# Modulation sums of two streams: one on VectorE, one on GpSimd, with GpSimd's transfers dealt out behind them

## The chip, the core and the metric

The program runs on one core of a Trainium2 chip. The core has a matmul engine (TensorE, PE in the profile), VectorE (DVE), ScalarE (ACT), GpSimd (POOL) and SyncE (SP), which here only issues transfers. The metric is device time of the program in microseconds (us). TensorE's clock is granted in two levels, 1.2 and 2.4 GHz; a stretch's granted clock of 1.00 means 2.4 GHz throughout.

## The reference, cut to what matters

Two layers of a block with three kinds of attention on a latent stream `x` and a context stream `ctx` (256 rows each, 2048 wide, float32), followed by a second block that the change doesn't touch. Each layer begins with a modulation: two vectors, one for each stream, are multiplied with the same matrix `w_ada[l]` of 2048 x 6144.

```python
sc = jax.nn.silu(c)
scc = jax.nn.silu(c_ctx)
shift, scale, gate = jnp.split(sc @ w_ada[l] + b_ada[l], 3, axis=-1)
shift_c, scale_c, gate_c = jnp.split(scc @ w_ada[l] + b_ada[l], 3, axis=-1)
h = rms(x, norm_w[l]) * (1.0 + scale[:, None]) + shift[:, None]
hc = rms(xc, norm_w[l]) * (1.0 + scale_c) + shift_c
u = h @ w_in          # for both streams, the same weights
x = x + gate[:, None] * merge_out(o_a, o_b, o_c, z, w_out[l])
```

The attention of kind A adds a bias table `rpb_a` of relative positions.

## The kernel before

**Weights.** All weight matrices stream through a ring of five slots in SBUF (`raw_ring`), 512 KB a chunk: 128 partitions x 1024 float32. SyncE issues the loads in one fixed order and waits before each for the slot's last user. A chunk of kind S (w_in, w_out) is split in two float32r parts: ScalarE casts it to `w_hi` (L666), VectorE subtracts to `w_lo` in place (L672), and TensorE multiplies three times (L703), 24 matmuls of 512 columns for four tiles of rows. VectorE prepares a chunk two ahead of the one that TensorE multiplies.

**Modulation blocks.** The matrices w_ada are cut in blocks of 512 columns, each of eight chunks. The first eight blocks run on TensorE at the start. The other 16 (numbers 8 to 23) are hosted: one chunk of w_ada (kind M) stands behind one chunk of kind S in the ring, as the list `PLACES` says. Twelve of these blocks serve both streams (`streams(n) == 2`): they lie behind win0 b 0 to 5, z0 b 1 to 3 and wout0 b 0 to 3, all in layer 0. The last four serve one stream, behind win1. For an M chunk VectorE does, in `dve_ada`, two halves of 512 columns, and in each half one instruction a stream: acc = chunk x silu_c + acc, with silu_c a scalar for each partition (L788; the first of a block is a plain product, L786). The accumulator `ACC` holds [128, 2 streams, 512]. The semaphore `mod_half` orders the halves, `mod_used` counts chunks and frees the slot for SyncE.

**The sum.** When a block's eight chunks are done, TensorE sums the accumulator over the partitions by 16 small matmuls with a vector of ones (`pe_ada_sum`, L768), in the middle of the weight chunk after next, and counts `ada_tr`. VectorE adds b_ada (L803).

**Around it.** In win0 b 0 to 2 and in wout0 the weight chunks follow each other directly. From win0 b 3 on, and in z0, they are dealt between the steps of the attention units (scores, VectorE's maximum, ScalarE's exponential, transposes, values). A block of w_out ends with `w_evac` on VectorE (L2732, L2734), four tiles.

**GpSimd** only issues transfers, in program order. `rpb_rows(l)` has 32 of 64 KB, made of rows of 256 bytes; layer 0's wait until win0's first block is evacuated, layer 1's until the gates are made (beginning of wout0). TensorE's `flip` needs all 32: in win0 b 2 for layer 0, in wout0 b 2 for layer 1. Then four transfers save x, one after each block of w_out (L631).

## Time and profile before

| | us |
|---|---|
| median of 3 runs | 3891.92 |
| lowest, highest | 3890.62, 3896.56 |
| the profiled execution | 3893.01 |
| its span, first to last instruction | 3891.2 |
| TensorE busy in it | 3647.3 (94%) |
| VectorE busy | 2013.7 (52%) |
| ScalarE busy | 1670.0 (43%) |
| GpSimd busy | 68.0 (2%) |

The profile of one execution has busy times of each engine, groups of instructions by line of the kernel with their mean duration, the idle time before them and what ended it, and an order of time. An arrow, as in "[3.97 <-DVE w_lo L672]", says that the engine was idle for 3.97 us and that VectorE's instruction at line 672 ended that. Idle time of an engine that nobody waits for costs nothing.

### The profile page before, as it was taken

How to read it: one execution, taken by the hardware profiler on the slowest of the kernel's cores; microseconds unless marked ns; L12 is line 12 of the kernel's file. 1: busy time of each engine (PE TensorE's matmuls, PEld its weight loads, DVE VectorE, ACT ScalarE, POOL GpSimd, SP SyncE). 2: the span in 40 equal slices, each digit the busy share in tenths (PEclk: the TensorE clock that was granted, in tenths of full speed). 3: DMA queues.
4: the chain of work that ended last, by engine and by line, in shares of the span. 5: the costliest groups of instructions: out<-in, count | busy, mean ns of one | idle time of the engine just before them, and what ended most of it. 6: DMA issues, size and time to landing. Idle time of an engine off the chain costs nothing.

```text
span 3891.2 us, 46277 instructions
## 1 busy us (share of the span) xinstructions
PE 3647.3 (94%) x18672; PEld 2943.5 (76%) x18672; DVE 2013.7 (52%) x3118; ACT 1670.0 (43%) x2696; POOL 68.0 (2%) x118
## 2 busy tenths in 40 slices
PE   7899999999898799999899999999999799999998
PEld 2677777887776677778677777766777599999776
DVE  1666654344567646642355544435455466666444
ACT  2323344434421423455544434444445555455433
POOL 1200000000020000000000000000000000000000
PEclk8999999999999999999999999999999999999999
DMA  9643322233364455223355566635555356666554
GB/s 363 187 146 114 98 60 55 58 103 100 108 191 150 134 173 179 87 64 108 93 180 160 160 178 178 179 103 159 179 173 178 103 163 186 188 185 188 180 184 162
DMA packets 351045, 577.49 MB, mean 148 GB/s; under 512 B 25316, under 2 KB 131060, under 8 KB 348912
## 3 DMA queue, kind: packets, MB, share of 16 engines
q1 hardware_dynamic: 344512, 549.47, 45.7%
q0 software_dynamic: 6320, 25.06, 2.3%
q8 instruction: 148, 2.42, 0.3%
q14 instruction: 65, 0.53, 0.0%
HBM read 570.26 MB, written 4.19 MB: 148 GB/s over the span
## 4 chain that ended last, share of the span: by engine, by line
PE 56%; DVE 4%; ACT 3%; DMA 2%; issue 1%; DVEq 0%; SPq 0%; ACTq 0%
PE ps L703 36%; PE ps L1576 13%; DVE w_lo L672 1%; PE ps L1272 1%; DMA raw_ring<-in_w_in_dram 1%; ACT w_hi L666 1%; PE ps L1076 1%; PE ps L1184 1%; PE ps L1453 1%; PE ps L1460 1%; PE ps L1157 1%; PE ps L1166 0%; PE ps L739 0%; DMA raw_ring<-in_w_proj_b_dram 0%; PE ps L1180 0%
## 5 line engine op out<-in xcount | busy, mean ns | idle before, releaser
L672 DVE TENSOR_TENSOR w_lo<-raw_ring,w_hi 128x1024 fp32r<-128x1024 f32 (+1 forms) x827 | 1007.0, 1223 | 1148.8 <-ACT w_hi L666 1147.6
L666 ACT CAST w_hi<-raw_ring 128x1024 fp32r<-128x1024 f32 (+1 forms) x827 | 861.0, 1047 | 1233.7 <-PE ps L703 518.0
L703 PE MATMUL ps<-w_hi,r_a 128*128 128x512 f32 x3552 | 1311.8, 408 | 54.2 <-DVE w_lo L672 22.3
L703 PE MATMUL ps<-w_lo,r_a 128*128 128x512 f32 (+1 forms) x2624 | 1040.8, 397 | 0.0
L703 PE MATMUL ps<-w_hi,r_b 128*128 128x512 f32 (+1 forms) x2272 | 864.7, 399 | 18.1 <-DVE w_lo L672 11.3
L703 PEld LDWEIGHTS ps<-w_hi,r_a 128*128 128x128 f32 x3552 | 676.7, 191 | 243.0 <-issue 64.2
L703 PEld LDWEIGHTS ps<-w_lo,r_a 128*128 128x128 f32 x2624 | 501.9, 191 | 114.1 <-issue 8.6
L703 PEld LDWEIGHTS ps<-w_hi,r_b 128*128 128x128 f32 x2272 | 436.7, 192 | 127.1 <-DVE w_lo L672 17.0
L1576 PE MATMUL ps<-r_a,w_hi 128*128 128x256 f32 x2816 | 498.7, 279 | 0.0
L1576 PEld LDWEIGHTS ps<-r_a,w_hi 128*128 128x128 f32 x2816 | 430.9, 188 | 0.0
L1576 PE MATMUL ps<-r_a,w_lo 128*128 128x256 f32 x1408 | 394.5, 280 | 0.0
L788 DVE SCALAR_TENSOR_TENSOR f_arena<-raw_ring,silu_c_t,f_arena 128x512 f32<-128x512 f32 x420 | 298.7, 747 | 3.7
L1576 PEld LDWEIGHTS ps<-r_a,w_lo 128*128 128x128 f32 x1408 | 264.7, 188 | 0.0
L703 PE MATMUL ps<-w_hi,act_t 128*128 128x512 f32 x704 | 224.0, 398 | 10.1 <-DVE w_lo L672 10.1
L1781 ACT COPY f_arena<-ps 128x512 f32<-128x512 f32 (+1 forms) x156 | 80.8, 518 | 244.0 <-PE ps L1166 243.7
L703 PEld LDWEIGHTS ps<-w_hi,act_t 128*128 128x128 f32 x704 | 133.5, 190 | 43.6 <-DVE w_lo L672 6.1
L1769 ACT ACTIVATE f_arena<-ps,neg_max 128x512 f32<-128x512 f32 (+1 forms) x156 | 97.0, 622 | 160.2 <-DVE neg_max L2547 119.1
L1272 PE MATMUL ps<-raw_ring,f_arena 128*128 128x192 f32 (+1 forms) x816 | 160.3, 354 | 3.1 <-ACT f_arena L1873 3.1
L2547 DVE TENSOR_REDUCE neg_max<-ps 128x1 f32<-128x512 f32 (+1 forms) x156 | 93.7, 601 | 126.3 <-PE ps L1151 89.6
L1272 PEld LDWEIGHTS ps<-raw_ring,f_arena 128*128 128x128 f32 x816 | 143.4, 192 | 14.5 <-ACT f_arena L1873 3.6
L703 PE MATMUL ps<-w_lo,act_t 128*128 128x512 f32 x352 | 140.1, 398 | 0.0
L1076 PE MATMUL ps<-consts,f_arena 128*128 128x128 f32 x508 | 81.9, 301 | 45.6 <-ACT f_arena L1700 14.2
(330 smaller groups left out, 2946.4 us busy)
## 6 DMA issues: line engine op xcount, KB each, us to landing
raw_ring<-in_w_in_dram SPq DMA_DIRECT2D x386, 512.0 KB, 3.7
raw_ring<-in_ffn_w_up_dram SPq DMA_DIRECT2D x176, 512.0 KB, 3.6
raw_ring<-in_w_ada_dram SPq DMA_DIRECT2D x128, 512.0 KB, 3.9
raw_ring<-in_w_out_dram SPq DMA_DIRECT2D x96, 512.0 KB, 3.7
raw_ring<-in_ffn_w_down_dram SPq DMA_DIRECT2D x88, 512.0 KB, 3.6
gla_arena<-in_w_ada_dram SPq DMA_DIRECT2D x64, 512.0 KB, 9.2
raw_ring<-in_w_proj_b_dram SPq DMA_DIRECT2D x32, 512.0 KB, 3.6
raw_ring<-in_w_proj_a_dram SPq DMA_DIRECT2D x16, 512.0 KB, 3.6
```

The lines of the kernel that those rows point to most:

```text
L666: nc.scalar.copy(WH[:, ph.s_slot(i, j), 0:n], RAW[:, ph.raw_slot(i, j), 0:n]).then_inc(hi_ready, 1)
L672: nc.vector.tensor_tensor(WL[:, ph.raw_slot(i, j), 0:n], RAW[:, ph.raw_slot(i, j), 0:n], WH[:, ph.s_slot(i, j), 0:n].bitcast(F32), ALU.sub ...
L703: mm = nc.tensor.matmul(PS[:, t, a:z], X(x, k, t), W[w][:, kk * cols + a:kk * cols + z], start=(k == 0 and q == 0), stop=(c == len(js) - 1 ...
L788: ins = nc.vector.scalar_tensor_tensor(acc[:, st, :], wk, SCT[:, k, st:st + 1], acc[:, st, :], ALU.mult, ALU.add)
L1076: return [lambda b, t=t: nc.tensor.transpose(PS[:, b, t * P:t * P + P], src(t), ident) for t in range(T)]
L1157: mm = nc.tensor.matmul(o, q[:, j, t * P:t * P + P], QKB[:, 3, kr], start=True, stop=True)
L1184: mm = nc.tensor.matmul(PS[:, 7, 0:HD], PTB[:, u % 2, q * P:q * P + P], U[:, kt, col:col + HD], start=(q == 0), stop=(q == len(kts) - 1))
L1272: mm = nc.tensor.matmul(PS[:, t, o:o + cols], X[:, k, t * P:t * P + P], RAW[:, ph.raw_slot(i, j), kk * cols:(kk + 1) * cols], start=(k == ...
L1576: mm = nc.tensor.matmul(PS[:, 4 * b + f, 0:256], W[w][:, kk * 256 + f % 2 * P:kk * 256 + f % 2 * P + P], HT[:, x, k, :], start=(k == 0 and ...
L1769: ins = nc.scalar.activation(pb[:, u % 2, 0:w], PS[:, 4 + u % 2, 0:w], ACT.Exp, bias=NM[:, u % 2:u % 2 + 1], accum_out=SUM[:, u % 2:u % 2 ...
L1781: nc.scalar.copy(pt[:, u % 2, 0:w], PS[:, 6, 0:w]).then_inc(pt_ready, 1)
L2547: mx = V.tensor_reduce(NM[:, q:q + 1], PS[:, 4 + q, 0:w], AX_X, ALU.max, negate=True)
```

## The change

VectorE keeps the first stream's sums and loses the second's. A new function `pool_ada` on GpSimd does the second stream for the 96 chunks of the twelve blocks with two streams: in each half a product into a temporary tile (`POOL_TMP`) and an addition into its half of the accumulator; a block's first half is only a product. Each of its instructions waits for a semaphore of the one before it (`pool_mul`, `pool_half`, `pool_mod`), and a block's first chunk waits until TensorE has summed the block before (`ada_tr`). SyncE now waits for `pool_mod` too before it reuses a slot of an M chunk, and TensorE for GpSimd's eighth chunk before the sum. `rpb_rows` takes a chunk number and issues 4 transfers instead of 32; these stand behind GpSimd's chunks of win0 b 1 and wout0 b 1. The saving of x stands behind the second chunk of the next block.

```diff
+        POOL_MODS = 96
...
                     sp.wait_ge({"S": pair_used, "P": plain_used, "M": mod_used}[k], n + 1)
+                    if k == "M":
+                        sp.wait_ge(pool_mod, min(n + 1, POOL_MODS))
...
+            def pool_ada(pool, n, ci, acc, tmp):
+
+                ph = PH[f"ada{ADAQ[n - 8][0]}"]
+                w = RAW[:, ph.raw_slot(n, ci)]
+                done = 8 * (n - 8) + ci
+                pool.wait_ge(raw_full[ph.raw_slot(n, ci)], ph.raw_full(n, ci))
+                if ci:
+                    pool.wait_ge(pool_mod, done)
+                else:
+                    pool.wait_ge(ada_tr, n)
+                for kk in range(2):
+                    k = 2 * ci + kk
+                    wk = w[:, kk * NB:(kk + 1) * NB].rearrange("p (a n) -> p a n", a=2)
+                    row = acc[:, 1, :].rearrange("p (a n) -> p a n", a=2)
+                    if k == 0:
+                        ins = nc.gpsimd.tensor_scalar(row, wk, SCT[:, k, 1:2], None, ALU.mult)
+                    else:
+                        nc.gpsimd.tensor_scalar(tmp, wk, SCT[:, k, 1:2], None, ALU.mult).then_inc(pool_mul, 1)
+                        pool.wait_ge(pool_mul, 2 * done + kk - (n - 8))
+                        ins = nc.gpsimd.tensor_tensor(row, row, tmp, ALU.add)
+                    if kk == 0:
+                        ins.then_inc(pool_half, 1)
+                        pool.wait_ge(pool_half, done + 1)
+                    else:
+                        ins.then_inc(pool_mod, 1)
...
-            pool.wait_ge(acc_free, AC["win0"][0][0] + 4)
-            rpb_rows(0)
-
+            pool.wait_ge(tr_free, TRN["h0"][0] + KT)
+            for b in range(6):
+                for c in range(8):
+                    mods("win0", b, c)
+                    if b == 1:
+                        if c == 0:
+                            pool.wait_ge(acc_free, AC["win0"][0][0] + 4)
+                        rpb_rows(0, c)
+            pool.wait_ge(o_evac, UN["c0"])
+            for b in range(1, 4):
+                for c in range(8):
+                    mods("z0", b, c)
             pool.wait_ge(tr_free, TRN["y0"][0] + KT)
             pool.dma_start(X4[:, 0:2], xin).then_inc(x_in, 16)
             pool.dma_start(X4[:, 2:4], cin).then_inc(x_in, 16)
-            pool.wait_ge(tr_free, TRN["gate0"][0] + 8)
-            rpb_rows(1)
             for b in range(4):
-                pool.wait_ge(acc_free, AC["wout0"][b][0] + 4)
-                pool.dma_start(xsv[:, :, NB * b:NB * b + NB], X4[:, 0:2, NB * b:NB * b + NB]).then_inc(x_saved, 16)
+                for c in range(8):
+                    mods("wout0", b, c)
+                    if b == 1:
+                        if c == 0:
+                            pool.wait_ge(tr_free, TRN["gate0"][0] + 8)
+                        rpb_rows(1, c)
+                    if b and c == 1:
+                        save_x(b - 1)
+            save_x(3)
...
             pe.wait_ge(mod_used, PH[f"ada{ADAQ[n - 8][0]}"].p(n, 7) + 1)
+            if streams(n) == 2:
+                pe.wait_ge(pool_mod, 8 * (n - 8) + 8)
...
-                for st in range(streams(n)):
-                    wk = w[:, kk * NB:(kk + 1) * NB]
...
+                wk = w[:, kk * NB:(kk + 1) * NB]
+                if k == 0:
+                    ins = nc.vector.tensor_scalar(acc[:, 0, :], wk, SCT[:, k, 0:1], None, ALU.mult)
+                else:
+                    ins = nc.vector.scalar_tensor_tensor(acc[:, 0, :], wk, SCT[:, k, 0:1], acc[:, 0, :], ALU.mult, ALU.add)
```

GpSimd's program before, from the last of the small loads to the saving of x; `f_arena<-in_rpb_a_dram` are the bias rows:

```order
L606 DMA gain_rows<-in_sink_b_dram 128x12
L620 DMA f_arena<-in_rpb_a_dram 64x4x64 [waits acc_free]
L620 DMA f_arena<-in_rpb_a_dram 64x4x64 x31
L625 DMA f_arena<-in_x_dram 128x2x2048 [waits tr_free]
L626 DMA f_arena<-in_ctx_dram 128x2x2048
```

The same engine in the changed program, behind win0 b 1, chunks 0 to 2; the second M chunk there is the last of a block, the third the first of the next, which waits for `ada_tr`:

```order
L645 TENSOR_SCALAR f_arena<-raw_ring,silu_c_t 128x512 [waits pool_mod,raw_full0]
L647 TENSOR_TENSOR f_arena<-f_arena 128x512 [waits pool_mul]
L645 TENSOR_SCALAR f_arena<-raw_ring,silu_c_t 128x512 [waits pool_half]
L647 TENSOR_TENSOR f_arena<-f_arena 128x512 [waits pool_mul]
L626 DMA f_arena<-in_rpb_a_dram 64x4x64 [waits acc_free]
L626 DMA f_arena<-in_rpb_a_dram 64x4x64 x3
L645 TENSOR_SCALAR f_arena<-raw_ring,silu_c_t 128x512 [waits pool_mod,raw_full2]
L647 TENSOR_TENSOR f_arena<-f_arena 128x512 [waits pool_mul]
L645 TENSOR_SCALAR f_arena<-raw_ring,silu_c_t 128x512 [waits pool_half]
L647 TENSOR_TENSOR f_arena<-f_arena 128x512 [waits pool_mul]
L626 DMA f_arena<-in_rpb_a_dram 64x4x64 x4
L643 TENSOR_SCALAR f_arena<-raw_ring,silu_c_t 128x512 [waits ada_tr,raw_full4]
```

The transfers moved from one piece ahead of everything else to places between the chunks, and each chunk brings four computing instructions. VectorE at a plain place of win0 b 0, one pair of chunks, before:

```order
L672 TENSOR_TENSOR w_lo<-raw_ring,w_hi 128x1024 [waits hi_ready]
L788 SCALAR_TENSOR_TENSOR f_arena<-raw_ring,silu_c_t,f_arena 128x512 [waits mod_used,raw_full1]
L788 SCALAR_TENSOR_TENSOR f_arena<-raw_ring,silu_c_t,f_arena 128x512
L788 SCALAR_TENSOR_TENSOR f_arena<-raw_ring,silu_c_t,f_arena 128x512 [waits mod_half]
L788 SCALAR_TENSOR_TENSOR f_arena<-raw_ring,silu_c_t,f_arena 128x512
```

and the same pair in the changed program:

```order
L726 TENSOR_TENSOR w_lo<-raw_ring,w_hi 128x1024 [waits hi_ready]
L843 SCALAR_TENSOR_TENSOR f_arena<-raw_ring,silu_c_t,f_arena 128x512 [waits mod_used,raw_full1]
L843 SCALAR_TENSOR_TENSOR f_arena<-raw_ring,silu_c_t,f_arena 128x512 [waits mod_half]
```

Two of four product sums are gone; the order of w_lo and M chunks is the same.

## Rows read from the trace of the kernel before

**Rows 1.** The page, busy time, share of the span and instructions of each engine.

```profile
PE 3647.3 (94%) x18672; PEld 2943.5 (76%) x18672; DVE 2013.7 (52%) x3118; ACT 1670.0 (43%) x2696; POOL 68.0 (2%) x118
```

**Rows 2.** Busy time by stretch: stretch, length, busy engines, granted clock, DMA share, GB/s.

```profile
119.00:258.00 139.00, 129.38 (x544) 101.46 (x543) 96.19 (x140) 40.91 (x61) 19.67 (x32) 0.97 0.57 156
258.00:430.00 172.00, 159.53 (x754) 126.25 (x753) 107.12 (x187) 59.74 (x110) 0.00 (x0) 0.96 0.41 122
430.00:690.00 260.00, 250.75 (x1280) 200.00 (x1279) 134.22 (x359) 119.91 (x270) 0.00 (x0) 0.98 0.22 61
690.00:1090.00 400.00, 376.54 (x1904) 314.15 (x1903) 181.79 (x373) 170.70 (x382) 1.42 (x2) 0.96 0.31 94
1090.00:1320.00 230.00, 198.34 (x834) 154.75 (x833) 154.88 (x225) 49.84 (x51) 22.52 (x36) 0.94 0.58 173
```

**Rows 3.** TensorE's waits in 119 to 1330 us: total, times, longest.

```profile
PE ps L703 <- DVE f_arena L2734: 14.1, 3, 6.1
PE ps L1166 <- ACT f_arena L1769: 11.7, 7, 2.7
PE ps L703 <- DVE w_lo L672: 8.3, 5, 4.0
PE ps L768 <- DVE f_arena L788: 5.4, 4, 2.7
```

**Rows 4.** Order of time in wout0 b 1: start, length, engine, line, operation.

```profile
1183.06 0.37 SPq L561 DMA_DIRECT2D raw_ring<-in_w_ada_dram  x1
...
1184.50 1.23 DVE L672 TENSOR_TENSOR w_lo<-raw_ring,w_hi 128x1024 fp32r<-128x1024 f32 x1 [2.10 <-ACT w_hi L666]
...
1185.65 2.86 DVE L788 SCALAR_TENSOR_TENSOR f_arena<-raw_ring,silu_c_t,f_arena 128x512 f32<-128x512 f32 x4
...
1188.66 0.37 SPq L561 DMA_DIRECT2D raw_ring<-in_w_ada_dram  x1
```

**Rows 5.** Groups by line: busy us, mean ns of one, idle before.

```profile
L786 DVE TENSOR_SCALAR f_arena<-raw_ring,silu_c_t 128x512 f32<-128x512 f32 x28 | 12.5, 481 | 0.0
...
L2306 DVE TENSOR_TENSOR r_b<-f_arena,r_a 128x512 fp32r<-128x512 f32 x32 | 22.2, 693 | 1.1
```

**Rows 6.** Order of time around the first burst of bias rows, and its busy stretch.

```profile
168.73 19.67 POOL L620 DMA_DIRECT2D f_arena<-in_rpb_a_dram  x32 [152.54 <-ACT f_arena L1728]
...
172.51 2.86 DVE L788 SCALAR_TENSOR_TENSOR f_arena<-raw_ring,silu_c_t,f_arena 128x512 f32<-128x512 f32 x4
...
183.01 1.05 ACT L666 CAST w_hi<-raw_ring 128x1024 fp32r<-128x1024 f32 x1 [12.95 <-DMA raw_ring<-in_w_in_dram]
...
195.21 0.50 PE L703 MATMUL ps<-w_hi,r_a 128*128 128x512 f32 x1 [3.97 <-DVE w_lo L672]
...
229.89 0.69 DVE L2396 TENSOR_TENSOR f_arena<-ps,consts 128x512 f32<-128x512 f32 x1 [5.24 <-PE ps L1107]
...
191.00:202.00 11.00, 7.03 (x25) 5.36 (x24) 6.83 (x9) 2.33 (x3) 0.00 (x0) 0.84 0.79 215
```

**Rows 7.** Sums and the second burst at the edges of blocks; two stretches.

```profile
179.72 1.84 PE L768 MATMUL ps<-one,f_arena 128*128 128x1 f32 x16
...
1133.81 19.65 POOL L620 DMA_DIRECT2D f_arena<-in_rpb_a_dram  x32 [50.27 <-ACT f_arena L1956]
...
1141.61 1.84 PE L768 MATMUL ps<-one,f_arena 128*128 128x1 f32 x16
...
1196.72 1.84 PE L768 MATMUL ps<-one,f_arena 128*128 128x1 f32 x16
...
1153.00:1164.00 11.00, 9.20 (x40) 7.14 (x39) 3.97 (x5) 1.44 (x2) 1.17 (x2) 1.00 1.03 277
1164.00:1175.00 11.00, 10.25 (x45) 7.96 (x44) 9.36 (x12) 2.75 (x3) 0.00 (x0) 1.00 0.59 182
```

**Rows 8.** The page, loads of w_ada by SyncE: count, KB each, us to landing.

```profile
raw_ring<-in_w_ada_dram SPq DMA_DIRECT2D x128, 512.0 KB, 3.9
```

34 lines of the change are left out of this document (19 added, 15 removed).

## The prediction

> **What bounds the kernel now.** I read the page's first two parts first, then the busy time by stretch, then the groups by line, and last the order of time around the places where work changes engine. TensorE is busy 94% of the span, VectorE 52%, GpSimd 2%, and GpSimd's 68.0 us are transfer issues [rows 1]. So the kernel is bound by TensorE, and VectorE's load can cost something only where TensorE stands still for it. The modulation chunks that are split here lie in four stretches of layer 0: 119 to 258, 258 to 430, 690 to 1090 and 1090 to 1320 us. TensorE is idle there for 9.6, 12.5, 23.5 and 31.7 us [rows 2]. The list of its waits in 119 to 1330 us names causes, here those that touch the work around the change [rows 3]: 14.1 us at w_out's evacuation, 11.7 us for the exponentials, 8.3 us for w_lo, and only 5.4 us, in 4 waits, for the last product sum of a modulation block (L788). That last item is the only one that the change takes away for certain.
>
> A plain stretch looks so [rows 4]: SyncE issues one chunk of w_ada and one of w_out or w_in every 5.60 us (1183.06, 1188.66), which is 24 matmuls of TensorE. In each pair VectorE does one w_lo (1.23 us) and four product sums (2.86 us): 4.1 of 5.6 us. It isn't late, it waits for ScalarE's w_hi.
>
> **The change part by part.**
> (1) VectorE loses two of four instructions in 96 chunks: 192 instructions, of which 12 are plain products. At 0.715 us (2.86 / 4, [rows 4]) that is 137 us of VectorE's time, nearly all beside TensorE's matmuls. On the path: the 5.4 us of waits for L788 [rows 3], and something in the stretch where attention runs between the weight parts. TensorE is idle 7.3% in 258 to 430 us, but 3.6% in 430 to 690 us, the same kind of work without modulation [rows 2]; 3.7% of 172 us is 6 us, and halving VectorE's share cannot give back more than about half. I book -6 us for both (bounds -11 and 0).
>
> (2) GpSimd gets for each chunk two products and two additions of 512 columns, each waiting for the one before it. The trace of before has no computation of that kind on GpSimd. The lower bound is VectorE's own rows [rows 5]: product 0.48, addition of two SBUF tiles 0.69, so 2 x 1.17 = 2.3 us a chunk. As the upper bound I take GpSimd at half VectorE's rate, the price of w_lo's 1024 columns for each of the four: 4 x 1.22 = 4.9 us. I use 4.3 us, near the upper end, as each of the four is started by a semaphore and none overlaps the next. The Trainium skill (GPSIMD Engine Reference, section 3.1, Elementwise — side-by-side cycle accounting) gives 769 ns for 512 elements of a one-input loop and 4497 ns for an addition of 2048; an estimate by it is 2 x (0.77 + 1.12) = 3.8 us and the waits, so the sum would be half a microsecond a chunk shorter. No run here shows it.
>
> (3) Both engines now read SBUF in the same microseconds. If they take turns, GpSimd also stands for VectorE's w_lo and its two remaining product sums: 1.15 + 2 x 0.71 = 2.6 us a pair. (1.15 is from the start of w_lo at 1184.50 to the next start, [rows 4].) So a chunk costs GpSimd between 4.3 and 6.9 us. What overlap the trace has speaks neither way: four product sums took 2.86 us at 172.51 while GpSimd issued transfers, and 2.86 us at 1185.65 while it did nothing [rows 4, 6], but an issue does not read operand tiles. I take 6.9, because every one of GpSimd's four and VectorE's three instructions in a pair has its operands in SBUF. The Trainium skill (SBUF — State Buffer, Who interferes with whom) says that a VectorE instruction with two SBUF inputs and a GpSimd instruction that reads SBUF hold the shared ports one at a time. By that rule it is 6.9, without it 4.3; it speaks against this change, and no row here can confirm it.
>
> (4) The new waits. SyncE may reuse a slot of w_ada only when GpSimd has finished too, and behind that wait all later weight loads are queued. TensorE's sum of a block waits for GpSimd's eighth chunk. GpSimd's first chunk of a block waits for the sum before (one half of the accumulator tile is its own). So each block has a loop: eight chunks on GpSimd, then TensorE's 1.84 us sum. 8 x 6.9 - 1.2 (the first chunk has no addition in its first half) + 1.8 = 56 us, against TensorE's own time per block: eight plain pairs of 5.60 us are 44.8 us, and with what lies between blocks the distance of two sums in w_out is 55.1 us (1141.61 to 1196.72) [rows 4, 7]. The first block has some 10 us of start ahead of it, as its first chunk is loaded before the stretch begins. I book +2 us for all blocks without transfers at 6.9 (0 at 4.3: 35 us a block hides under 44.8).
>
> (5) The transfers of rpb_a. Before, 32 of them stand in one burst of 19.67 us, 0.61 us each, at 168.73 and at 1133.81 [rows 6, 7]. The first burst delays weight loads: ScalarE waits 12.95 us for one, TensorE stands 3.97 us at 195.21 and runs 191 to 202 us at a granted clock of 0.84 [rows 6]. I price the first burst at 6.5 us and the second, where TensorE is busy 9.20 and 10.25 of 11 us, at 2.5 us [rows 6, 7]. Dealt out, four issues (2.46 us) stand behind each of eight chunks, and these chunks cost GpSimd 6.8 us without turns and about 8.7 with them (some of VectorE's work falls beside the issues). Two blocks decide:
> First block, win0 b 1: TensorE's sum starts at 179.72 and GpSimd begins its next block at about 181.5 [rows 7]. One short chunk (5.6 + 2.5) and five of 8.7: 233; 3 us to land (the eight times larger weight loads take 3.9, [rows 8]); the first flip, which needs all 32, comes at 236, and its copy stood at 229.89 [rows 6]. +6 us.
> Second block, w_out b 1: begins at 1143.4, where the sum of 1141.61 ends [rows 7]; 8.1 + 7 x 8.7 + 0.9 for the saved rows, less the last 2.5: GpSimd is done at 1211, and TensorE's next sum stood at 1196.72 [rows 7]. +14 us.
>
> Sum against the profiled execution: 3893.0 us (span 3891.2 and 1.8 around it) + 6 + 14 + 2 - 6 = 3909. The median of the runs shown is 1.1 lower, so 3908 us.
>
> **The rivals.**
> R1, no turns, GpSimd at 4.3 us. Speaks for it: the transfer issues didn't slow VectorE [rows 6]. Block win0 b 1: 181.5 + 3.2 + 2.5 + 5 x 6.8 + 3 = 224, flip 5 us earlier than now. w_out b 1: 1143.4 + 5.7 + 7 x 6.8 - 2.5 = 1194, inside 1196.72, so the burst's 2.5 us come back. With the relief of VectorE taken at 4 us: -11.5, 3880 us.
> R2, no turns, GpSimd at 4.9 us: flip at 228 (-1.5), w_out b 1 done at 1198 (+2), relief -4: 3888 us, no difference to be measured.
> R3, this one far on the slower side: turns, and VectorE loses as many of them. A w_lo that waits for two additions (2 x 1.2 us) eats most of what TensorE's lead of two chunks leaves, and the burst's queue behind SyncE adds. From about 7.5 us a chunk every one of the 12 blocks is GpSimd's: 8 x (8.0 - 6.9) = 9 us a block in six tight blocks above my sum: 3908 + 54 = 3962 us.
> R4, the change doesn't spread anything: acc_free stands ahead of the first transfers, and if GpSimd is late all its transfers are late; that is within the +6 and +14 above.
>
> **How the numbers follow.** Forecast 0.50 (3908, its own range 3895 to 3935), R1 0.25, R2 0.15, R3 0.10. A measurement of this kernel can tell about 0.2% (7.8 us) from no change: faster ends at 3884.1, slower begins at 3899.7. Forecast gives slower 0.37 and same 0.13 (with GpSimd nearer 3.8 us the two blocks shrink by 3 and 4 us); R1 gives faster 0.19, same 0.06; R2 same 0.12, faster 0.03; R3 slower. Together faster 0.22, same 0.31, slower 0.47. The range leaves out R3 and the best end of R1: 3877 to 3935.
>
> **What would show it.** Right: VectorE's product sums 240 instead of 420 and about 137 us less busy; GpSimd near 350 to 420 us busy more, its starts inside a chunk 1.1 to 1.7 us apart, and longer where w_lo lies beside; TensorE's largest new wait at L703 or the sum, on GpSimd, in w_out b 1; no burst of transfers, and no 12.95 us wait of ScalarE. The step on turns is wrong if GpSimd's additions last the same with and without VectorE beside them, or if the whole of VectorE's w_lo stay at 1.22 us and the chunk takes under 5 us. The relief is wrong if TensorE is as idle as now between 258 and 430 us. Wrong altogether if a block of GpSimd is over 60 us in the attention stretches.

## The result, and the profile after

The changed kernel takes 3958.64 us (median of 4 runs, 3957.27 to 3963.34) against 3891.32 us of the kernel before in the same job (4 runs, 3890.62 to 3896.56). The ratio is 1.0169, with a 95% interval of 1.0154 to 1.0183. The forecast was 3908 us. It had the sign, but the loss is 67 us where 16 were booked, and the time lies outside the range. Of the cases worked out, R3 (3962 us, chance 0.10) is nearest by its number.

Page of the kernel after, busy time, share of the span and instructions of each engine:

```profile
PE 3661.5 (93%) x18672; PEld 2947.8 (75%) x18672; DVE 1995.0 (50%) x2926; ACT 1669.6 (42%) x2696; POOL 684.1 (17%) x490
```

Against [rows 1], VectorE has 192 instructions fewer, as it should, but is only 18.7 us less busy (2013.7 - 1995.0), not 137. GpSimd is 616 us busier, not 350 to 420. The groups by line say why (behind the bar busy us and mean ns of one):

```profile
L645 POOL TENSOR_SCALAR f_arena<-raw_ring,silu_c_t 128x512 f32<-128x512 f32 x180 | 336.6, 1870 | 114.0 <-DMA raw_ring<-in_w_ada_dram 95.9 <-POOL f_arena L647 8.1
L647 POOL TENSOR_TENSOR f_arena<-f_arena 128x512 f32<-128x512 f32 x180 | 259.4, 1441 | 15.0
```

The next rows are durations of one line or tile by their least, median and largest (ns): GpSimd's product and addition, VectorE's product sum of the modulation, and its w_lo in 119 to 1330 us, all of the kernel after.

```profile
L645 POOL TENSOR_SCALAR f_arena<-raw_ring,silu_c_t x180: 1564/1575/3466, 116.2 to 1365.7; 128x512 f32<-128x512 f32 x180
L647 POOL TENSOR_TENSOR f_arena<-f_arena x180: 1261/1294/2387, 119.7 to 1367.4; 128x512 f32<-128x512 f32 x180
L843 DVE SCALAR_TENSOR_TENSOR f_arena<-raw_ring,silu_c_t,f_arena x180: 736/988/1805, 133.8 to 1358.1; 128x512 f32<-128x512 f32 x180
L726 DVE TENSOR_TENSOR w_lo<-raw_ring,w_hi x123: 1210/1226/2343, 124.8 to 1324.4; 128x1024 fp32r<-128x1024 f32 x123
```

And the same two lines of VectorE in the kernel before, where GpSimd computes nothing:

```profile
L788 DVE SCALAR_TENSOR_TENSOR f_arena<-raw_ring,silu_c_t,f_arena x373: 740/746/755, 131.4 to 1395.5; 128x512 f32<-128x512 f32 x187
L672 DVE TENSOR_TENSOR w_lo<-raw_ring,w_hi x129: 1207/1225/1229, 123.9 to 1320.0; 128x1024 fp32r<-128x1024 f32 x129
```

Before, both have the same duration to within 2%. After, the least values are those of an undisturbed instruction and the longest are 1.9 to 2.5 times as long; of VectorE's sums the median too went from 746 to 988 ns. The two engines' instructions stretch where they meet.

Not all of VectorE's do. Its maxima, which read TensorE's result in PSUM, are as long as before (first line before, second after), and so are the instructions of w_evac (L2788: 686 to 689 ns, before 686 to 690):

```profile
L2547 DVE TENSOR_REDUCE neg_max<-ps x104: 411/554/693, 289.9 to 1054.3; 128x1 f32<-128x512 f32 x52, 128x1 f32<-128x256 f32 x52
```

```profile
L2601 DVE TENSOR_REDUCE neg_max<-ps x104: 408/552/694, 310.1 to 1079.8; 128x1 f32<-128x512 f32 x52, 128x1 f32<-128x256 f32 x52
```

Busy time by stretch in the kernel after, in the columns of [rows 2]:

```profile
119.00:258.00 139.00, 115.87 (x465) 90.49 (x463) 85.70 (x91) 38.76 (x59) 120.37 (x93) 0.91 0.53 140
258.00:430.00 172.00, 157.59 (x753) 124.47 (x753) 98.03 (x146) 55.23 (x98) 132.85 (x81) 0.98 0.40 122
690.00:1090.00 400.00, 371.09 (x1876) 308.75 (x1874) 171.65 (x324) 168.27 (x383) 153.75 (x93) 0.97 0.29 89
1090.00:1320.00 230.00, 188.37 (x775) 145.21 (x776) 133.60 (x143) 41.41 (x52) 183.07 (x133) 0.90 0.51 148
```

In the first stretch TensorE gets through 465 matmuls instead of 544, in the last through 775 instead of 834, and its granted clock fell from 0.97 to 0.91 and from 0.94 to 0.90. GpSimd is busy 120 of 139 us and 183 of 230 us: where weight chunks follow each other directly, it has next to no slack left.

The next list is TensorE's longest waits (total, times, longest) and answers to [rows 3]. The same work ends 61.5 us later, so it goes from 119 to 1391 us:

```profile
PE ps L757 <- DVE f_arena L2788: 27.2, 3, 9.5
PE ps L1341 <- DVE f_arena L2429: 23.3, 3, 9.6
PE ps L757 <- DVE w_lo L726: 22.3, 11, 4.4
PE ps L757 <- ACT f_arena L1782: 13.9, 2, 10.9
PE ps L1220 <- ACT f_arena L1823: 12.8, 8, 2.9
PE ps L824 <- POOL f_arena L647: 9.1, 2, 6.9
```

L2788 is w_evac, L2429 the rotation of q and k, L1782 ScalarE's evacuation in w_in and L1823 the exponentials; before, these waits were 14.1, 17.2, 4.1 and 11.7 us, and w_lo's 8.3. TensorE waits for GpSimd itself only 9.1 us, 6.9 of them at the last sum of w_out. GpSimd is late more often in another place, at the ring of weight slots. In SyncE's queue of waits (119 to 1400 us) this row is new:

```profile
SPq L565 <- POOL f_arena L647: 255.1, 51, 9.3
```

51 times SyncE stands for GpSimd until it may load a slot again. With five slots and two kinds of chunk in turn, a slot that held a chunk of w_ada mostly gets a weight chunk next: of 48 loads that start within 0.15 us of the end of a GpSimd addition, 41 are of w_in or w_out. So it is TensorE's own chunk that is held up: GpSimd's addition ends at 211.64, and the load of w_in is issued at 211.71.

```profile
210.13 1.51 POOL L647 TENSOR_TENSOR f_arena<-f_arena 128x512 f32<-128x512 f32 x1
211.71 0.37 SPq L568 DMA_DIRECT2D raw_ring<-in_w_in_dram  x1
```

At a block's edge such a late chunk costs more than itself. ScalarE's cast and VectorE's w_lo of it stand in the program ahead of the evacuation of the finished block, for which TensorE waits:

```profile
1240.34 1.41 DVE L726 TENSOR_TENSOR w_lo<-raw_ring,w_hi 128x1024 fp32r<-128x1024 f32 x1 [6.20 <-ACT w_hi L720]
1241.67 0.69 DVE L2786 TENSOR_TENSOR ps<-ps,f_arena 128x512 f32<-128x512 f32 x1
```

So the lost time shows up as waits for whoever prepares the late chunk or stands behind it (w_lo, w_evac, ScalarE's evacuation L1782), and little of it under GpSimd's name.

The order of time in win0 b 1 (start, length, engine, line) shows one loop of a chunk with four transfers:

```profile
201.69 2.50 POOL L626 DMA_DIRECT2D f_arena<-in_rpb_a_dram  x4
204.23 1.93 POOL L645 TENSOR_SCALAR f_arena<-raw_ring,silu_c_t 128x512 f32<-128x512 f32 x1
206.24 1.29 POOL L647 TENSOR_TENSOR f_arena<-f_arena 128x512 f32<-128x512 f32 x1
207.63 2.42 POOL L645 TENSOR_SCALAR f_arena<-raw_ring,silu_c_t 128x512 f32<-128x512 f32 x1
210.13 1.51 POOL L647 TENSOR_TENSOR f_arena<-f_arena 128x512 f32<-128x512 f32 x1
211.58 2.50 POOL L626 DMA_DIRECT2D f_arena<-in_rpb_a_dram  x4
```

211.58 - 201.69 = 9.89 us for a pair of chunks whose matmuls take TensorE 5.6 us. VectorE in the same microseconds:

```profile
206.84 1.77 DVE L726 TENSOR_TENSOR w_lo<-raw_ring,w_hi 128x1024 fp32r<-128x1024 f32 x1 [2.11 <-ACT w_hi L720]
208.53 1.96 DVE L843 SCALAR_TENSOR_TENSOR f_arena<-raw_ring,silu_c_t,f_arena 128x512 f32<-128x512 f32 x2
```

w_lo took 1.77 us, not 1.23, and two sums 1.96 us, not 1.43 (half of 2.86, [rows 4]). GpSimd's product that lies beside both took 2.42 us, not 1.57. Each gives the other part of its time; neither stops for the whole of the other's instruction.

And one whole block of w_out, from one sum to the next: first the 55 us of the kernel before, then the 76 us of the kernel after (columns as above: length, busy time of PE, PEld, DVE, ACT, POOL, granted clock, DMA share, GB/s).

```profile
1142.00:1197.00 55.00, 48.79 (x209) 38.68 (x209) 36.41 (x49) 8.39 (x8) 12.73 (x21) 0.97 0.72 189
```

```profile
1172.00:1248.00 76.00, 54.89 (x209) 42.84 (x208) 33.21 (x33) 7.34 (x7) 71.30 (x64) 0.84 0.62 143
```

Both hold the same 209 matmuls. Of the 21 us, 6.1 are TensorE's own work at a lower clock (54.89 - 48.79, granted 0.84 instead of 0.97) and 14.9 are idle time (21.1 instead of 6.2 us). GpSimd is busy 71.3 of 76 us.

### The profile page after: what moved, and what is told of

The parts are those of the page before. It is cut to its first block, busy times and chain, and to the rows that moved or that the text cites. A ratio compares the mean times of both kernels' runs of the same rounds, so it can differ in the third digit from the quotient of the medians.

```text
span 3955.8 us, 46689 instructions
## 1 busy us (share of the span) xinstructions
PE 3661.5 (93%) x18672; PEld 2947.8 (75%) x18672; DVE 1995.0 (50%) x2926; ACT 1669.6 (42%) x2696; POOL 684.1 (17%) x490
## 3 DMA queue, kind: packets, MB, share of 16 engines
q8 instruction: 148, 2.42, 0.3%
## 4 chain that ended last, share of the span: by engine, by line
PE 55%; DVE 4%; ACT 3%; DMA 2%; issue 1%; DVEq 0%; SPq 0%; ACTq 0%
PE ps L757 35%; PE ps L1630 13%; DVE w_lo L726 1%; PE ps L1326 1%; DMA raw_ring<-in_w_in_dram 1%; ACT w_hi L720 1%; PE ps L1130 1%; PE ps L1238 1%; PE ps L1507 1%; PE ps L1514 1%; PE ps L1211 1%; PE ps L1220 0%; PE ps L793 0%; DMA raw_ring<-in_w_proj_b_dram 0%; PE ps L1234 0%
## 5 line engine op out<-in xcount | busy, mean ns | idle before, releaser
L726 DVE TENSOR_TENSOR w_lo<-raw_ring,w_hi 128x1024 fp32r<-128x1024 f32 (+1 forms) x827 | 1038.9, 1261 | 1226.9 <-ACT w_hi L720 1225.7
L645 POOL TENSOR_SCALAR f_arena<-raw_ring,silu_c_t 128x512 f32<-128x512 f32 x180 | 336.6, 1870 | 114.0 <-DMA raw_ring<-in_w_ada_dram 95.9
L647 POOL TENSOR_TENSOR f_arena<-f_arena 128x512 f32<-128x512 f32 x180 | 259.4, 1441 | 15.0
L843 DVE SCALAR_TENSOR_TENSOR f_arena<-raw_ring,silu_c_t,f_arena 128x512 f32<-128x512 f32 x240 | 233.5, 973 | 3.7
L1823 ACT ACTIVATE f_arena<-ps,neg_max 128x512 f32<-128x512 f32 (+1 forms) x156 | 97.1, 622 | 166.9 <-DVE neg_max L2601 124.9
```

The costliest lines, as they stand in the source:

```text
L645: nc.gpsimd.tensor_scalar(tmp, wk, SCT[:, k, 1:2], None, ALU.mult).then_inc(pool_mul, 1)
L647: ins = nc.gpsimd.tensor_tensor(row, row, tmp, ALU.add)
L726: nc.vector.tensor_tensor(WL[:, ph.raw_slot(i, j), 0:n], RAW[:, ph.raw_slot(i, j), 0:n], WH[:, ph.s_slot(i, j), 0:n].bitcast(F32), ALU.sub ...
L843: ins = nc.vector.scalar_tensor_tensor(acc[:, 0, :], wk, SCT[:, k, 0:1], acc[:, 0, :], ALU.mult, ALU.add)
L1823: ins = nc.scalar.activation(pb[:, u % 2, 0:w], PS[:, 4 + u % 2, 0:w], ACT.Exp, bias=NM[:, u % 2:u % 2 + 1], accum_out=SUM[:, u % 2:u % 2 ...
```

## The experiments

The table gives, for each kernel, how many microseconds later than in the kernel before the same matmul (by its number in the program) starts, at moments of the kernel before. 110 to 250 us is w_in's first part, 250 to 680 attention and what follows, 680 to 1090 the z part, 1090 to 1330 w_out. From 1330 on no block with two streams is left. The text calls these numbers the lag. They compare one profiled execution of each kernel, and repeated executions of the kernel before lie up to 15 us apart in these jobs, so a time from a single run is no better than that.

```
before, us       110    150    190    250    300    430    680   1090   1140   1210   1330   1600   2180   2420
after           -0.6   -0.4    6.7   17.8   19.2   16.6   18.3   23.3   29.4   50.9   61.5   60.6   60.0   66.8
sums_only       -0.3    1.0   26.8   25.7   26.6   26.7   28.1   32.3   38.6   53.8   64.6   63.6   63.7   63.6
off_ring        -0.1    1.2   10.3   21.1   19.8   20.1   19.7   25.9   26.3   48.2   53.3   53.0   52.7   56.3
rpb_sp          -1.0    0.0    3.2    4.0    4.8    5.0    4.5   11.2   24.9   33.7   45.1   44.5   44.2   51.4
no_dve_sums     -0.6   -0.4    6.1   14.0   12.1    8.5    8.1   11.9   15.5   36.5   41.7   40.8   40.7   40.6
shadow           1.8    3.1   11.9   14.7   17.9   23.6   26.7   34.3   38.5   44.4   53.7   52.3   52.1   52.1
half_pool        0.3    1.6    0.4   -1.0   -4.3   -7.9  -10.5   -7.6   -6.8   -4.2   -5.4   -7.3   -7.4   -7.4
split_cols      -0.6    0.2    0.8   -0.0   -1.4   -1.2   -2.3   -2.2   -2.2    3.0    3.8    4.0    3.3   10.1
split_sp         0.4    1.5    4.6    5.7    3.8    4.9    4.5    2.7   14.8   15.0   15.7   13.3   13.0   13.0
deal_only        0.4    1.1   -0.2   -1.5   -1.6   -1.9   -2.9   -3.5   -2.9   -1.9   -1.7   -1.9   -2.5    4.3
attn_only        4.0    4.0    3.1    3.9    3.9    1.7    2.6    6.3    6.8    6.4    6.9    7.3    6.4   13.2
```

The 3.6 to 7.2 us that six of the eleven gain between 2180 and 2420 us lie in layer 1, in short falls of the granted clock. deal_only, whose time is that of the kernel before, has them, and sums_only, as slow as the changed kernel, has not. I don't count them to the change. The 4 us of attn_only at 110 us lie ahead of everything that it changes.

### deal_only: the transfers dealt, the sums not moved

```diff
-        POOL_MODS = 96
+        POOLB = ()
...
+                        pool.wait_ge(mod_used, 8 * (b - 1) + c + 7)
                         rpb_rows(0, c)
...
+                        pool.wait_ge(mod_used, 64 + 8 * b + c + 1)
                         rpb_rows(1, c)
```

VectorE does both streams; GpSimd issues four transfers after each of VectorE's chunks.

> VectorE keeps both streams' sums as before; GpSimd computes nothing. Only the bias rows are dealt out: four transfers behind each chunk of win0 b 1 and of wout0 b 1, each four paced by VectorE's count of finished w_ada chunks. If the burst costs what the prediction booked (6.5 and 2.5 us), this comes out 9 us below before, 3882 us, and ScalarE's 12.95 us wait for a load is gone. Rival: the weight loads lose as much to eight small packets of bias rows as to one burst, or the later arrival of the 32nd transfer holds the first flip: 3891 us or a few us more.

Measured: 3894.17 us against 3897.39 (ratio 0.9994, interval 0.9984 to 1.0004). ScalarE's waits for weight loads in 150 to 230 us add up to 51.1 us in deal_only (11 waits, the longest 8.3 us) and to 50.5 in the kernel before (10, 12.9). The 12.95 us wait of [rows 6] is gone, but their sum is the same, and the table shows 1.5 us won at 250 and 1.9 at 1210 us. Between the table's moments more is won: the lag goes from 1.0 us at 180 to -5.9 at 203 us, so the first burst did cost about the 6.5 us at which it was priced. But 4.4 us are lost again at the block's edge. There a load of w_in is late, ScalarE casts its chunk before it evacuates the finished block, and TensorE waits for that 5.4 us, where it waited 2.2 before:

```profile
216.71 1.04 ACT L727 CAST w_hi<-raw_ring 128x1024 fp32r<-128x1024 f32 x1 [5.02 <-DMA raw_ring<-in_w_in_dram]
218.87 0.77 PE L764 MATMUL ps<-w_hi,r_a 128*128 128x512 f32 x1 [5.39 <-ACT f_arena L1791]
```

The DMA share in 202 to 213 us is 0.99, where it was 0.59: the dealt transfers probably make the load late, which no run shows by itself. In w_out it is the same on a smaller scale, 1.9 us won by 1170 and 2.3 lost by 1197 us. So the bursts had a price, but dealing moves it to another place instead of giving it back.

### attn_only: GpSimd sums in blocks 11 to 15 alone

```diff
-        POOL_MODS = 96
+        POOLB = (11, 12, 13, 14, 15)
...
+            pool.wait_ge(acc_free, AC["win0"][0][0] + 4)
+            for x in range(8):
+                rpb_rows(0, x)
```

These are the blocks between attention units and in z, where GpSimd has time; the transfers are in bursts as before.

> GpSimd sums the second stream of five blocks only, 11 to 15, those behind win0 b 3 to 5 and z0, where attention runs between the weight parts; the other seven are VectorE's as before, and the bias rows go in one burst as before. Theory 1 (relief is real where a pair of chunks takes longer than GpSimd's 7 us): 2 to 6 us below before, 3886 to 3889 us. Theory 2 (VectorE's instructions with two SBUF operands are stretched by GpSimd's, and they stand ahead of the maxima that attention waits for): 3 to 8 us above before, 3895 to 3900 us.

Measured: 3901.22 us against 3897.39 (ratio 1.0015, 1.0004 to 1.0026), 4 to 6 us above, which fits theory 2. In 250 to 430 us it wins 2.2 us, in 680 to 1090 it loses 3.7. The 6 us of relief are not there. Two waits of TensorE in z before, alone and with GpSimd beside:

```profile
PE ps L1287 <- DVE f_arena L2375: 17.2, 3, 7.2
```

```profile
PE ps L1346 <- DVE f_arena L2434: 23.3, 3, 9.6
```

Here TensorE stands for the last addition of the rotation of q and k, a chain of small VectorE instructions. One such addition takes 291 to 293 ns in the kernel before and up to 1262 ns in the kernel after. The 6.1 us more of this wait are about the 5 us that the changed kernel loses in z. All seven such additions together are only 1 us longer, though, and in shadow none of them is; most of the growth must lie ahead of them in the chain, as in a product of 128x256 (L2662; L2716 after) that went from 0.42 to up to 1.48 us. The same wait is 17.2 us in deal_only, 19.2 in split_cols, 20.7 in half_pool, 21.3 in shadow, and 23.2 to 23.4 in each other kernel in which GpSimd sums the whole second stream in z: it grows with GpSimd's load.

### half_pool: GpSimd leaves out the second half of each chunk

```diff
-                for kk in range(2):
+                for kk in range(1):
```

The second stream's sums lack the second 128 rows of every chunk; GpSimd does half as many instructions, VectorE as in the changed kernel.

> The changed kernel, but GpSimd leaves out the second half of each chunk (every odd product and addition of the second stream), so it needs about 3 to 3.5 us a chunk instead of 6.1 to 7. Theory 1 (the 67 us are GpSimd's lateness): nearly all of it goes, 3890 to 3897 us, since 3.5 + 2.5 us is about a pair's 5.6 us. Theory 2 (the cost is that both engines read SBUF at once): half of the overlap is left, so about half of the loss, 3920 us or more.

Measured: 3882.33 us in one run, 0.9961 of 3897.39, and faster than either theory had it. TensorE no longer waits for GpSimd at all, and VectorE's lighter load shows: from 250 to 680 us the lag goes from -1.0 to -10.5 us. GpSimd's instructions still take 1718 and 1352 ns on average. This run does less than the kernel has to, so it isn't a version; it says that the loss goes when GpSimd has half as much to do.

### off_ring: GpSimd holds no slot

```diff
-                        sp.wait_ge(pool_mod, min(n + 1, POOL_MODS))
+                        held = 0
...
-                    wk = w[:, kk * NB:(kk + 1) * NB].rearrange("p (a n) -> p a n", a=2)
+                    wk = CN[:, 0:NB].rearrange("p (a n) -> p a n", a=2)
```

The products read a tile of constants instead of the chunk (the second stream's modulation is then meaningless), at the same size and in the same order, and SyncE no longer waits for GpSimd.

> The changed kernel, but GpSimd's products read a fixed tile of constants instead of the chunk (its sums are of other numbers), and SyncE no longer waits for GpSimd before it reuses a slot. What is left is the loop of a block: TensorE's sum waits for GpSimd's eighth chunk, GpSimd's next block for the sum. Theory 1 (held slots starve w_hi, w_lo and TensorE chunk by chunk, and make the loss larger than the loop): 3915 us or less. Theory 2 (the loop alone sets it): within 8 us of the changed kernel, 3950 to 3960 us, with the waits moved from w_lo to the sum.

Measured: 3947.02 us in one run, near theory 2 and 3 us below its range. Of the loss 50 of 67 us stay. The waits only change their place (119 to 1383 us, the same work):

```profile
PE ps L830 <- POOL f_arena L651: 33.4, 3, 16.9
PE ps L1169 <- issue: 16.1, 1, 16.1
```

The first is TensorE at the sum, for GpSimd. The second is the first flip, for which the program waits until all 32 bias transfers are in. w_lo, 22.3 us in the changed kernel, is down to 4.3. So the slots that GpSimd holds are where the delay shows, and cost some 8 us beyond it at 1330 us (61.5 - 53.3); the cause is GpSimd's chain itself: eight chunks and the sum form a loop longer than the block's matmuls, and in two blocks the issues lengthen it. The constants' tile made GpSimd no faster (1883 and 1416 ns), so the ring, which the weight loads are written to, is not what slows it.

### rpb_sp: SyncE issues the bias rows

```diff
+                if ph is PH["win0"] and i == 1 and j >= 4:
+                    if j == 4:
+                        sp.wait_ge(acc_free, AC["win0"][0][0] + 4)
+                    for x in (2 * j - 8, 2 * j - 7):
+                        rpb_rows(sp, 0, x)
+                if ph is PH["wout0"] and i == 1:
+                    if j == 0:
+                        sp.wait_ge(tr_free, TRN["gate0"][0] + 8)
+                    rpb_rows(sp, 1, j)
```

> The changed kernel, but SyncE issues the bias rows, between its weight loads (eight transfers behind each of win0 b 1's chunks 4 to 7, four behind each of wout0 b 1's), and GpSimd none. Theory 1 (a block is a loop of GpSimd's eight chunks and TensorE's sum, and the four issues of 2.5 us lengthen it from 56 to 71 us in each of two blocks): 25 to 35 us less than the changed kernel, 3925 to 3935 us, what is left being eight chunks of 7 us against 45 to 55 us. Theory 2 (the loss comes from held slots and the two engines' common use of SBUF, whoever issues the rows): 3945 us or more.

Measured: 3942.01 us in one run, 48 above 3893.99; 17 to 19 less than the changed kernel, and between the two theories. In w_in the lag at 250 us is 4.0, not 17.8: GpSimd's issues were 14 of the 18 us there. In w_out the 21.5 us of 1140 to 1210 become 8.8, but 13.7 instead of 6.1 stand in 1090 to 1140, at a block's edge, where SyncE waits for the gates before its first issue:

```profile
PE ps L763 <- DVE f_arena L2796: 31.8, 3, 16.2
```

So the issues' cost is on whoever has a chain that nothing may wait in, and in w_out SyncE is such an engine too.

### no_dve_sums: VectorE's own sums cut to 8 of 512 columns

```diff
+                NV = NB - 8 if n in POOLB else 0
...
+                        ins = nc.vector.scalar_tensor_tensor(acc[:, st, NV:], wk[:, NV:], SCT[:, k, st:st + 1], acc[:, st, NV:],
+                                                              ALU.mult, ALU.add)
```

The first stream's modulation is left out but for 8 columns, so that GpSimd meets only w_lo and the rest of VectorE's work.

> The changed kernel, but VectorE's sums of the first stream in the twelve blocks are cut to 8 of 512 columns (the first product of a block stays whole), so that of VectorE's instructions with two SBUF operands in a pair only w_lo is left beside GpSimd. If the engines take turns, GpSimd's products and additions come near their undisturbed 1.57 and 1.26 us (now 1.87 and 1.44 in the mean), a chunk takes 6.2 instead of 7 us, and the time falls by 0.8 us for each chunk of the tight blocks, some 30 to 40 us: 3920 to 3930 us. If GpSimd alone is slow: above 3945 us.

Measured: 3933.66 us in one run (1.0102 of 3893.99), between the two cases expected. GpSimd's pair of instructions went from 1870 and 1441 to 1780 and 1403 ns, a chunk from 6.6 to 6.4 us. At 1330 us the lag is 41.7 instead of 61.5, with 6.4 of the 19.8 us won between 250 and 680. Even with hardly any sum on VectorE two thirds of this lag remain. The 19.8 us are not the price of meetings alone, since this edit takes VectorE's own time for the sums away too. Its 8-column sums last

```profile
L850 DVE SCALAR_TENSOR_TENSOR f_arena<-raw_ring,silu_c_t,f_arena x180: 214/227/1280, 133.8 to 1338.1; 128x8 f32<-128x8 f32 x180
```

with a mean of 472 ns: an instruction of 0.23 us that meets GpSimd can wait 1 us. The price of a meeting is not in proportion to the size of the instruction that is held up.

### split_cols and split_sp: GpSimd takes 256 of the second stream's 512 columns

```diff
+        PC = 256
...
-                    wk = w[:, kk * NB:(kk + 1) * NB].rearrange("p (a n) -> p a n", a=2)
-                    row = acc[:, 1, :].rearrange("p (a n) -> p a n", a=2)
+                    wk = w[:, kk * NB:kk * NB + PC]
+                    row = acc[:, 1, 0:PC]
...
+                for st in range(streams(n)):
+                    o = PC if st and n in POOLB else 0
```

VectorE sums the other 256. split_sp has SyncE's issues of rpb_sp besides.

> All twelve blocks, but GpSimd sums only the first 256 of the second stream's 512 columns, VectorE the other 256; bias rows dealt out as in the changed kernel. GpSimd needs about 3.5 us a chunk, 6 with issues. Theory 1 (GpSimd's lateness is the whole loss, and the relief of VectorE is real, as the kernel with half of GpSimd's work showed with 3882 us): 3882 to 3890 us. Theory 2 (that kernel was fast because second-stream work was left out): 3892 to 3900 us.

> As the one with split columns, and the bias rows issued by SyncE, none by GpSimd. If GpSimd's loop still sets something in the two blocks with issues, 2 to 6 us less than with split columns on GpSimd; if not, the same within 3 us.

Measured: split_cols 3902.53 us (ratio 1.0022, 1.0010 to 1.0034), 2.5 us above the range of its theory 2; split_sp 3904.64 us (1.0027, 1.0017 to 1.0037), the same within 3 us. GpSimd in split_cols:

```profile
L651 POOL TENSOR_SCALAR f_arena<-raw_ring,silu_c_t 128x256 f32<-128x256 f32 x180 | 210.3, 1169 | 228.1 <-DMA raw_ring<-in_w_ada_dram 215.6 <-POOL f_arena L653 2.6
L653 POOL TENSOR_TENSOR f_arena<-f_arena 128x256 f32<-128x256 f32 x180 | 165.4, 919 | 15.0
```

Half the columns cost 63% of the time, 4.2 us a chunk instead of 6.6. That fits into TensorE's 5.6 us, and 58 of the 67 us are gone. But nothing is won: the lag is -2.2 us at 1090, lost again in w_out b 1 where four issues are added to each chunk. With SyncE's issues the edge of the block in w_out costs 12 us (2.7 to 14.8), and the wait for w_evac has a longest of 15.8 us, as in rpb_sp.

### shadow: only the sharing

```diff
-                        sp.wait_ge(pool_mod, min(n + 1, POOL_MODS))
...
-                    row = acc[:, 1, :].rearrange("p (a n) -> p a n", a=2)
+                    wk = CN[:, 0:NB].rearrange("p (a n) -> p a n", a=2)
+                    row = tmp
...
-            if streams(n) == 2:
+            if n in (12, 15, 19):
                 pe.wait_ge(pool_mod, 8 * (n - 8) + 8)
...
+                for st in range(streams(n)):
```

> In this kernel VectorE sums both streams as before, and GpSimd does the second stream's products and additions once more beside it, on the constants' tile and a tile of its own, with a result that nobody reads. SyncE and TensorE don't wait for it, but for one wait in the last block of each of the three stretches; the bias rows are issued in bursts, the first one chunk of w_ada later than before. So only the shared way to SBUF is left of the change, at more load than in the changed kernel, since VectorE keeps its 192 sums. Theory 1 (the loss is the waits for a slow GpSimd; the sharing by itself is worth little to TensorE): 3895 to 3912 us; VectorE's product sums are stretched from 0.72 to about 1 us, but TensorE still has most of its lead. Theory 2 (VectorE is stretched so far by the sharing that TensorE's waits for w_lo alone cost 20 us or more): 3920 us or more, and the loss grows evenly through the attention stretches.

Measured: 3944.05 us (median of 4 runs; ratio 1.0119, 1.0100 to 1.0139). Nobody uses what GpSimd computes, and it costs 47 us. Theory 1 of its expectation is wrong, theory 2 holds, but for the even growth: 9 us are lost in 250 to 430, 8 in 680 to 1090, 19 in 1090 to 1330. TensorE's waits in 119 to 1330 us (to 1384 us these four stay the same):

```profile
PE ps L762 <- DVE w_lo L731: 23.5, 13, 5.7
PE ps L1348 <- DVE f_arena L2436: 21.3, 3, 9.1
PE ps L762 <- DVE f_arena L2795: 19.7, 3, 8.0
PE ps L1227 <- ACT f_arena L1830: 17.6, 11, 3.8
```

Against [rows 3] w_lo has gained 15 us, the exponentials 6, w_evac 6. One wait is of my making, 11.3 us for GpSimd at the last sum of a stretch. It costs about 6 us in the end: behind it TensorE waits 7.2 us for ScalarE where the kernel before waits 14.2. So some 40 us are the sharing's. This is more than in the changed kernel, since VectorE keeps four sums a pair: 4 x 0.98 + 1.34 us of w_lo (the means in 119 to 1330 us) are 5.3 us of TensorE's 5.6, where it had 4.1 before.

### sums_only: the changed kernel with the issues in bursts

```diff
-                    if b == 1:
-                        if c == 0:
-                            pool.wait_ge(acc_free, AC["win0"][0][0] + 4)
-                        rpb_rows(0, c)
+                    if (b, c) == (1, 0):
+                        pool.wait_ge(acc_free, AC["win0"][0][0] + 4)
+                        for x in range(8):
+                            rpb_rows(0, x)
```

> The changed kernel with the bias rows in bursts again: 32 issues in a row behind the first chunk of win0 b 1, and 32 in a row behind the last chunk of wout0 b 0. If the dealt issues are costly because each four of them stand before a chunk of GpSimd's (issues are additive on GpSimd, wherever they stand), the time stays within 8 us of the changed kernel's 3958, since 32 issues take 20 us in the same two blocks; SyncE then stands about 20 us at once and TensorE runs out of weights there. If dealing itself (one wait per chunk, descriptors beside weight loads) did the harm, this kernel is 10 us or more faster, under 3948.

Measured: 3956.64 and 3966.07 us, the time of the changed kernel (ratio to before 1.0161, 1.0139 to 1.0184). The lag jumps at once by 20 us at 190, as TensorE stands at the sum:

```profile
204.21 3.54 PE L829 MATMUL ps<-one,f_arena 128*128 128x1 f32 x16 [19.06 <-POOL f_arena L652]
```

and at 1330 us it is 64.6 against 61.5. That is the first case of its expectation. Dealing the transfers neither helps nor harms by more than some 3 us: 32 issues add their 20 us to GpSimd's chain wherever they stand.

## Why the prediction was wrong

Two steps of the sum failed. The relief of VectorE, booked at -6 us, did not come, because the forecast let GpSimd pay for the shared SBUF and VectorE not. And the price of GpSimd's blocks on TensorE's path was too small, +2 us for ten blocks and +6 and +14 for the two with transfers, against 16.7 (in three blocks of w_out alone), 17.8 and 21.5 us by the lag. The length of a chunk on GpSimd, from which both prices were worked out, came out right by luck.

**What bounds the kernel.** Right: TensorE is the bound, and GpSimd becomes a second one in w_in and w_out. TensorE's waits grew most for w_lo, w_evac and ScalarE's evacuation, not for GpSimd as the signs had it. The test for "wrong altogether", a block of over 60 us in the attention stretches, was no test: two sums lie 61 to 107 us apart there in the kernel before already. Outside them w_out b 1 has 76 us.

**(1) Relief, booked at -6 us: absent.** The step took VectorE's durations from a trace in which GpSimd computes nothing, and subtracted 192 of them. The rest got longer by nearly as much: the sums from 747 to 973 ns, w_lo in its meetings up to 2343 ns, and VectorE's busy time fell by 18.7 us instead of 137. The prediction's own sign for this says the same: TensorE is idle 14.4 us in 258 to 430, where it was 12.5. In 250 to 680 us the lag grows by 0.5 us, and in z it grows by 5.0, where the sum had nothing. half_pool shows a relief of 9.5 us in 250 to 680, but it leaves a quarter of the sums out altogether; split_cols, with as much on GpSimd and the rest on VectorE, wins 2.3 us there.

**(2) GpSimd's own time, taken as 4.3 us with 4.9 as the upper bound: wrong, it is 6.1.** Product and addition have medians of 1.575 and 1.294 us. Undisturbed halves start 198.81 - 195.77 = 3.04 us apart in win0 b 1:

```profile
195.77 1.57 POOL L645 TENSOR_SCALAR f_arena<-raw_ring,silu_c_t 128x512 f32<-128x512 f32 x1
197.43 1.28 POOL L647 TENSOR_TENSOR f_arena<-f_arena 128x512 f32<-128x512 f32 x1
198.81 1.57 POOL L645 TENSOR_SCALAR f_arena<-raw_ring,silu_c_t 128x512 f32<-128x512 f32 x1
```

The bound was a guess in the form of a row: half of VectorE's rate. For the addition it nearly held (1.29 for VectorE's 0.69), for the product it did not (1.57 for 0.48). The Trainium skill (GPSIMD Engine Reference, section 3.1) had been weighed with 0.77 us for a product of 512; the measured 1.57 us decides. For the chances this was the worst step, since R1 and R2 (0.25 and 0.15) stood on it: with 6.1 us neither can occur.

**(3) The turns, booked at 2.6 us a chunk: mechanism right, size wrong.** The engines slow each other, but by part of an instruction. GpSimd's mean chunk is 2 x (1.87 + 1.44) = 6.6 us and with the gaps 7.0, so the sharing adds some 0.9 us. The Trainium skill (SBUF — State Buffer, Who interferes with whom) has the two engines hold the shared ports one at a time; shadow confirms that they get in each other's way, while 1.77 us for w_lo beside a product of 2.42 us is less than whole turns would make it. The forecast's 6.9 us a chunk is thus almost the measured 7.0, by two errors that cancel. What it left out is the other side. VectorE loses time to GpSimd too, and some of that work lies on TensorE's path: w_lo and the rotation. The maxima and w_evac kept their lengths; w_evac is waited for longer because it stands behind a late chunk's w_lo. VectorE's loss is R3's mechanism, to which I gave 0.10 with the price put into GpSimd's chunk (8.0 us), where it isn't. shadow comes nearest to measuring it alone: some 40 us with VectorE's full load. In the changed kernel, no_dve_sums takes 20 us out by removing a part of it, and with it VectorE's time for the sums.

**(4) The loop of a block, booked at +2 us for all but two blocks.** Taken at 1140 and 1330 us, w_out b 0, b 2 and b 3 lost 6.1 + 10.6 us, and the first block in w_in 6.7 by 190 us. Eight chunks of 7.0 us and the sum leave no slack against 55.1 us, and the held slots make the edges of the blocks dearer. The largest single loss is in the last block, for which the step had the wrong number. It set GpSimd's 56 us against 55.1 us everywhere, but the trace of the kernel before has the sums of w_out at 1141.61, 1196.72, 1258.16 and 1301.94: the last distance is 43.8 us, as no edge of a block lies in it. In the kernel after, these sums are at 1312.06 and 1368.78, 56.7 us apart:

```profile
1301.94 1.84 PE L768 MATMUL ps<-one,f_arena 128*128 128x1 f32 x16
```

```profile
1368.78 3.54 PE L824 MATMUL ps<-one,f_arena 128*128 128x1 f32 x16 [6.91 <-POOL f_arena L647]
```

So the lag grows by 12.9 us in that block alone, from 53.9 to 66.8. Of these 5.3 come back at once, as TensorE waits 7.2 us for ScalarE behind this sum instead of 14.2.

**(5) The two blocks with transfers, booked at +6 and +14.** The bursts' prices, 6.5 and 2.5 us, are about what deal_only wins at first (6.9 and 1.9), but most of that is lost again at the block's edge. split_cols, whose GpSimd needs 4.2 us a chunk, as R1 supposed, has 3.0 us of lag at 1210 us and not R1's gain. A chunk with four issues was booked at 8.7 us and takes 8.5 to 9.9 in w_in and 8.4 to 10.2 in w_out. In w_in the forecast put GpSimd's start of the block at 181.5 and the flip at 236; they are at 188.34 and 245.95:

```profile
188.34 1.65 POOL L643 TENSOR_SCALAR f_arena<-raw_ring,silu_c_t 128x512 f32<-128x512 f32 x1
...
239.86 2.50 POOL L626 DMA_DIRECT2D f_arena<-in_rpb_a_dram  x4
...
245.95 1.58 PE L1161 MATMUL ps<-f_arena,consts 128*128 128x512 f32 x2 [2.22 <-issue]
```

6.8 us later at the start, and five chunks 0.6 us longer each, make the 10 us by which the flip is late on the forecast. The step was sound in form; its two inputs were not, the late start (the block before is GpSimd's too) and the chunk. The rest of the 17.8 us is the 6 that were booked, 1 us because the forecast set the flip against its copy (229.89) and not against the flip's own matmul, at 228.83 in the kernel before, and under 1 us at a lower clock. Most of it stands ahead of the flip, though: at the block's edge, 236.51, TensorE waits 10.9 us for ScalarE's evacuation behind a late weight chunk, a path that the prediction doesn't name. The two overlap. Without held slots (off_ring) the flip alone makes TensorE wait 16.1 us. In w_out b 1 the distance of two sums is 76.25 us (1171.35 to 1247.60) against 55.1, so +21.1 for +14: GpSimd needs 71 us from its first product to its last addition where 67.6 was booked, and the sum comes 3 us after that, behind a wait of 9.5 us for w_evac.

**The account at 1330 us**, forecast and measured: w_in to 250 us +6, +17.8; 250 to 680 us -6, +0.5; z 0, +5.0; w_out b 0 0, +6.1; b 1 +14, +21.5; b 2 and b 3 +2, +10.6. Together +16 and +61.5. Of the second number GpSimd's issues are some 16 (against rpb_sp, whose own issues cost something again), VectorE's first-stream sums and GpSimd's meetings with them 20, and held slots 8; these overlap and can't be added. How the rest divides between GpSimd's own slowness and the sharing with w_lo stays open: to separate them a GpSimd as slow as this would be needed that doesn't touch SBUF, which was not tried. What the clock adds lies inside all the shares, as the 6.1 of 21 us in w_out b 1 show.

No variant that computes everything beats the kernel before; the nearest that uses GpSimd for sums at all, attn_only, is at 1.0015.

## What to carry to other kernels

Work that is handed to an idle engine must be priced at that engine's own row for that operation and size. Where there is none, the range has to be wide enough to change the verdict, and a rule like "half the rate" is no bound. Then price the donor again: VectorE's remaining instructions were longer by almost all that it had given away, and some of those on TensorE's path were among them. When a slow engine shares a ring, look for it in the loading queue's waits, since the engine that stands still names somebody else, and ask which load comes next into the slot that it holds. Price a loop against each block's own length, the shortest one first.
